# A two-layer diffusion block with a product-key expert layer: a group of four tokens weighed one token later, with ten ring slots

## The chip, the cores and the metric

One core of a Trainium2 chip. The time is that of one launch on the device in microseconds (us), from the runs shown; one execution is also profiled. Engines: TensorE (PE), VectorE (DVE), ScalarE (ACT), GpSimd (POOL) and SyncE (SP), which issues most weight loads. TensorE's clock has two levels, 1.2 and 2.4 GHz; a granted clock of 0.5 is the lower one.

## The reference

Two layers over 256 latent tokens with a context of 256 tokens, width 1024, all in float32. Each layer has a mixer (convolution, two kinds of attention, a Fourier mix, merged by gates) and then a layer of experts that is chosen by product keys. In the first layer the context tokens go through both; in the second only the latent ones do. So three sets of 256 tokens go through the experts, here called turns. The part that matters here is the end of the expert layer:

```
v1, i1 = top_k(s1, 16); v2, i2 = top_k(s2, 16)          # per token and head (8 heads)
cand = v1[..., :, None] + v2[..., None, :]
top_s, pos = top_k(cand, 16); eidx = cidx[pos]          # 16 of 16384 experts per head
g = softmax(top_s)
h = gelu(einsum('thkd,td->thk', eu[eidx], xc))          # 128 rows of 1024 per token
out = einsum('thk,thkd->td', g * h, ev[eidx])           # 128 more rows of 1024
```

For each token 128 experts are chosen. The rows `eu` of these are multiplied with the token and summed (128 numbers), the gelu of that times the softmax gives 128 weights, and the weighted sum of the 128 rows `ev` is the token's result.

## The kernel before

**Rows of experts.** A ring of ten slots (`SLOTS`) holds the rows of one token each: 128 partitions, one per chosen expert, with 1024 numbers of `eu` and 1024 of `ev`, 1 MB in all. GpSimd requests a token's rows with an indirect transfer (`ask`, L748) into slot `token % 10`. Before that it waits until the group whose token held the slot has been weighed (semaphore `weighed`).

**Per token.** TensorE broadcasts the token's 1024 numbers over the partitions of PSUM, in two halves of 512 (L1389; the operand `xr` holds the token as three bfloat16 parts, loaded by ScalarE's queue at L1827, two groups ahead). VectorE multiplies each half with the `eu` rows and sums it (L2535, which here is called a dot; it has two halves). The banks of the broadcast are a single pair, so a half of the next broadcast waits for the same half of the dot before (`dotted`). Only in the last 128 tokens of the third turn are there two pairs in turn (`x_bank`), and a broadcast waits for the dot two tokens back.

**Per group of four tokens.** After the fourth dot VectorE adds the halves (L2540), ScalarE takes the gelu (L1839), and VectorE multiplies with the softmax (L2545, `zcol`; semaphore `w_s`). VectorE waits for ScalarE in between and then goes on to the first dot of the next group. `weigh(g)` on TensorE is the weighted sum: eight matmuls with a weight of 32 columns (L1370), two halves for each of four tokens, that add to banks 6 and 7. Its last matmul raises `weighed`, which lets GpSimd request four more tokens. At the end of 32 groups (a tile of 128 tokens) ScalarE copies the sum out.

**Order.** Each engine's program is written out in a fixed order by a weaver (`Weave`): the steps of the layers (products, attention, norms, selection of experts) come in the order of `SCRIPT`, and between them tokens of the expert stream (`experts`) are put in, as many as the step's entry in `SHARE` grants. TensorE, VectorE, ScalarE and GpSimd use the same sequence, each with its part of a step and of a token. So a token stands between two steps of the layer, and where the steps have run out (`after` in the script) tokens follow each other directly. An engine works through its program in order: whatever stands behind a waiting instruction waits too.

Of the kernel before, what the change touches and what calls it, by code (L numbers as in the profile page):

```python
# [47 lines left out]
NR = NG // TT  # L48
# [177 lines left out]
def build(nc, x, ctx, ccols, cols_c, w_ada, w_rows, w_in, w_gate, w_out, w_q, w_key, b_in, nat_bias, gqa_sink, peer_uv0, peer_uv1,  # L226
          ident_c, wave_c, band_c, iota_c, strip_c, out):
    es = ExitStack()
    with es:
# [137 lines left out]
        def bank(i, a=0, b=512):  # L367
            return PS[:, i * 512 + a:i * 512 + b]
# [83 lines left out]
        def slot_of(q, n):  # L452
            whole = q * TOK + n
            return whole % SLOTS, 16 * (whole // SLOTS + 1)
# [34 lines left out]
        def x_bank(q, n):  # L489

            return 2 * (n % 2) if ORDER[q] == LAT1 and n >= P else 0
# [272 lines left out]
        def _(pe):  # L764
# [592 lines left out]
            def experts():  # L1357
                for q, f in enumerate(ORDER):
                    b = OF[f]
                    a = at_of["back", b]  # L1360

                    def weigh(g):
                        pe.wait_ge(w_s, q * NG + g + 1)
                        at = g % NR
                        if at == 0 and (q or g):
                            pe.wait_ge(y_out, 2 * q + g // NR)
                        for h in range(2):
                            for k in range(GRP):
                                slot, _ = slot_of(q, g * GRP + k)
                                last = T.matmul(PS[k * NR:(k + 1) * NR, (6 + h) * 512:(7 + h) * 512],  # L1370
                                                zcol[:, g % 2, k, NR - 1 - at:2 * NR - 1 - at],
                                                ring[:, slot, D + h * 512:D + (h + 1) * 512],
                                                start=(at == 0), stop=(at == NR - 1))
                        last.then_inc(weighed, 1)

                    for n in range(TOK):
                        g, k = n // GRP, n % GRP
                        whole = q * TOK + n
                        if n == 0:
                            pe.wait_ge(a["sel_s"], a.at("sel_s", 2))  # L1380
                        if k == 0:
                            pe.wait_ge(xr_land[g % 2], 16 * (q * NG // 2 + g // 2 + 1) * GRP)
                        for h in range(2):
                            if whole:
                                turns = 1 if n and x_bank(q, n) != x_bank(q, n - 1) else 0
                                if whole > turns:
                                    pe.wait_ge(dotted, 2 * (whole - turns) - 1 + h)
                            p0 = 32 * ((k + h) % GRP)
                            T.matmul(bank(x_bank(q, n) + h), onesb[p0:p0 + 3, :],  # L1389
                                     xr[p0:p0 + 3, g % 2, h * 512:(h + 1) * 512], start=True, stop=True)\  # L1390
                                .then_inc(xb_s, 1)
                        if k == 0 and g % NR:
                            weigh(g - 1)
                        if k == GRP - 1 and g % NR == NR - 1:
                            weigh(g)
                        yield
# [4 lines left out]
            for s_ in range(2):  # L1401
# [3 lines left out]
                last.then_inc(crow_p, 1)  # L1405
            woven["pe"] = Weave()
            woven["pe"].run(dict(ada=ada, norm=norm, front=front, early=early, part=part_, back=back, residual=residual), experts())

        @block.scalar
# [1269 lines left out]
```

## Time and profile before

| | |
|---|---|
| median of 3 runs | 3026.46 us (3022.73 to 3033.0) |
| profiled execution, its own time | 3031.7 us |
| its span in the trace | 3029.9 us |
| TensorE's mean granted clock | 0.785 |
| moved by the DMA engines | 1029.85 MB, mean 340 GB/s |
| requests of expert rows | 768, 805.36 MB |

How to read it. The span is the time from the first to the last recorded instruction. The busy time of an engine is the time in which it had at least one instruction in work; a share of 79% is an average over parts of the program with different limits. For a group of instructions, the idle time before them tells how long the engine had stood still, and the releaser is what ended most of that. The chain of waits starts at the last instruction and goes back to what released it. The DMA share is the mean busy share of the 16 DMA engines; at 1.0 a further transfer has to queue.

The three turns of the expert stream lie at about 470 to 1310 us, 1350 to 2110 us and 2320 to 3013 us. Up to 470 us and from 2140 to 2310 us no tokens are in work. From about 2460 us to the end there is next to nothing but tokens.

### The profile page before, as it was taken

How to read it: one execution, taken by the hardware profiler on the slowest of the kernel's cores; microseconds unless marked ns; L12 is line 12 of the kernel's file. 1: busy time of each engine (PE TensorE's matmuls, PEld its weight loads, DVE VectorE, ACT ScalarE, POOL GpSimd, SP SyncE). 2: the span in 40 equal slices, each digit the busy share in tenths (PEclk: the TensorE clock that was granted, in tenths of full speed). 3: DMA queues.
4: the chain of work that ended last, by engine and by line, in shares of the span. 5: the costliest groups of instructions: out<-in, count | busy, mean ns of one | idle time of the engine just before them, and what ended most of it. 6: DMA issues, size and time to landing. Idle time of an engine off the chain costs nothing.

```text
span 3029.9 us, 34666 instructions
## 1 busy us (share of the span) xinstructions
PE 2392.9 (79%) x11912; PEld 1305.4 (43%) x11912; DVE 1918.9 (63%) x6197; ACT 452.5 (15%) x1108; POOL 729.4 (24%) x779
## 2 busy tenths in 40 slices
PE   7989996878999878568989978878797566676556
PEld 6778892444556435113545543322685111121111
DVE  3879977876545557856864455665458855555555
ACT  2141120223100110012010012221221000000000
POOL 0000003232322222322322223332001333333332
PEclk8999996888999978667989987675898555655565
DMA  8628748998999988978999999999434989999996
GB/s 329 246 84 330 300 178 334 373 359 324 398 419 414 387 332 327 350 311 319 388 417 419 421 384 383 393 385 367 183 137 190 368 341 418 402 379 418 403 404 282
DMA packets 155375, 1029.85 MB, mean 340 GB/s; under 512 B 19136, under 2 KB 29888, under 8 KB 34496
## 3 DMA queue, kind: packets, MB, share of 16 engines
q0 software_dynamic: 110592, 805.36, 66.0%
q1 hardware_dynamic: 31648, 209.70, 17.7%
q10 hardware_dynamic: 12960, 12.59, 1.2%
q8 instruction: 94, 1.54, 0.2%
q14 instruction: 81, 0.66, 0.1%
HBM read 1018.66 MB, written 8.91 MB: 339 GB/s over the span
## 4 chain that ended last, share of the span: by engine, by line
PE 54%; DMA 19%; DVE 19%; issue 3%; ACT 2%; POOL 1%; ACTq 1%; SPq 0%; DVEq 0%; POOLq 0%
DMA ring<-in_peer_uv,eT 17%; PE PS L1370 14%; DVE ring L2535 9%; PE PS L930 7%; PE PS L1389 7%; PE PS L852 4%; PE PS L1041 4%; PE PS L951 2%; PE PS L971 2%; PE PS L1014 2%; DMA xr<-xrows 2%; PE PS L1223 1%; PE PS L854 1%; PE PS L815 1%; PE PS L1123 1%
## 5 line engine op out<-in xcount | busy, mean ns | idle before, releaser
L2535 DVE CUSTOM_DVE_ANT_0 ring<-ring,PS 128x512 f32<-128x512 f32 x1536 | 993.9, 685 | 783.3 <-PE PS L1389 600.5
L748 POOL DMA_INDIRECT ring<-in_peer_uv,eT x768 | 727.7, 947 | 2269.6 <-PE PS L1370 1422.2
L1389 PE MATMUL PS<-xr,onesb 3*128 3x512 bf16 x1536 | 527.7, 480 | 429.1 <-DVE hcol L2535 337.0
L1370 PE MATMUL PS<-ring,zcol 128*32 128x512 f32 x3072 | 579.1, 893 | 96.2 <-DVE zcol L2545 94.2
L1389 PEld LDWEIGHTS PS<-xr,onesb 3*128 3x128 bf16 x1536 | 105.2, 95 | 959.9 <-DVE hcol L2535 484.9
L1370 PEld LDWEIGHTS PS<-ring,zcol 128*32 128x32 f32 x3072 | 102.7, 142 | 379.2 <-issue 218.0
L930 PE MATMUL PS<-uT,W 128*128 128x256 f32 x1024 | 249.3, 393 | 0.0
L1839 ACT ACTIVATE ge<-hdot 128x4 f32<-128x4 f32 x192 | 39.4, 205 | 1263.0 <-DVE hdot L2540 1262.9
L930 PEld LDWEIGHTS PS<-uT,W 128*128 128x128 f32 x1024 | 193.6, 194 | 48.7 <-issue 22.2
L1912 DVE CUSTOM_DVE_ANT_0 ring<-ring 128x1024 f32<-128x1024 f32 x160 | 190.2, 1221 | 7.6 <-DMA ring<-in_w_rows 3.5
L852 PE MATMUL PS<-uT,W 128*128 128x256 f32 (+1 forms) x672 | 156.0, 386 | 8.6 <-ACT uT L1453 8.2
L852 PEld LDWEIGHTS PS<-uT,W 128*128 128x128 f32 x672 | 122.7, 200 | 41.8 <-issue 17.1
L971 PE MATMUL PS<-uT,W 128*128 128x256 f32 x512 | 133.5, 405 | 0.0
L2535 DVE DVE_READ_ACCUMULATOR2_ANT hcol<- 128x1 f32 x1536 | 126.6, 82 | 0.0
L1041 PE MATMUL PS<-uT,ring 128*128 128x128 f32 x1024 | 120.7, 280 | 5.7 <-DVE scratch L2388 5.7
L1041 PEld LDWEIGHTS PS<-uT,ring 128*128 128x128 f32 x1024 | 119.0, 196 | 6.1 <-DVE scratch L2388 6.1
L971 PEld LDWEIGHTS PS<-uT,W 128*128 128x128 f32 x512 | 95.7, 197 | 37.3 <-issue 26.1
L951 PE MATMUL PS<-mix,W 128*128 128x256 f32 x320 | 81.0, 385 | 0.0
L1941 DVE SCALAR_TENSOR_TENSOR mix<-hpad,cols,mix 128x256 f32<-128x256 f32 x180 | 77.5, 480 | 0.3
L1534 ACT ACTIVATE hpad<-PS,cols 128x256 f32<-128x256 f32 x64 | 30.4, 476 | 275.4 <-PE PS L951 274.3
L2545 DVE TENSOR_TENSOR zcol<-ge,gT 128x4 f32<-128x4 f32 x192 | 32.2, 167 | 58.9 <-ACT ge L1839 58.9
L951 PEld LDWEIGHTS PS<-mix,W 128*128 128x128 f32 x320 | 61.8, 194 | 9.7 <-issue 1.0
(362 smaller groups left out, 2287.0 us busy)
## 6 DMA issues: line engine op xcount, KB each, us to landing
ring<-in_w_rows SPq DMA_DIRECT2D x40, 1024.0 KB, 8.0
W<-in_w_in SPq DMA_DIRECT2D x30, 1024.0 KB, 9.5
W<-in_w_gate SPq DMA_DIRECT2D x16, 1408.0 KB, 8.0
W<-in_w_gate SPq DMA_DIRECT2D x16, 1280.0 KB, 7.7
W<-in_w_out SPq DMA_DIRECT2D x20, 1024.0 KB, 6.0
W<-in_w_gate SPq DMA_DIRECT2D x16, 1152.0 KB, 10.4
ring<-in_w_q SPq DMA_DIRECT2D x16, 1024.0 KB, 13.9
ring<-in_peer_uv,eT POOLq DMA_INDIRECT x768, 12.7
```

The lines of the kernel that those rows point to most:

```text
L748: pool.indirect_dma_start(ring[:, slot, :], None, (peer_uv0, peer_uv1)[b.l], bass.IndirectOffsetOnAxis(eT[:, f % 2, t:t + 1], 0)).then_inc ...
L852: last = T.matmul(bank(2 + n % 4, 0, r.nt * P), wk[:, blk * P:(blk + 1) * P], u_[:, k, r.cols], **go)
L930: T.matmul(bank(2 + n % 4, 0, TOK), wg[:, k, n % 2, :], uT[:, k, :], start=(k == 0), stop=(k == KD - 1))
L951: last = T.matmul(bank(2 + n % 4, TOK, 2 * TOK), W[:, slot, TILE + (at - first_kt + k) * P:TILE + (at - first_kt + k + 1) * P], yb[:, at + ...
L971: last = T.matmul(bank(2 + n % 4, 0, TOK), wg[:, k, g % 2, :], uT[:, k, :], start=(k == 0), stop=(k == KD - 1))
L1014: last = T.matmul(out_bank(m), W[:, slot, k * 2 * P + n % 2 * P:k * 2 * P + (n % 2 + 1) * P], mT[:, k, tt * P:(tt + 1) * P], start=(k == 0 ...
L1041: last = T.matmul(bank(2 + u % 2, 0, P), ring[:, u // 2, w0:w0 + P], uT[:, k, tt * P:(tt + 1) * P], start=(k == 0), stop=(k == KD - 1))
L1370: last = T.matmul(PS[k * NR:(k + 1) * NR, (6 + h) * 512:(7 + h) * 512], zcol[:, g % 2, k, NR - 1 - at:2 * NR - 1 - at], ring[:, slot, D + ...
L1389: T.matmul(bank(x_bank(q, n) + h), onesb[p0:p0 + 3, :], xr[p0:p0 + 3, g % 2, h * 512:(h + 1) * 512], start=True, stop=True)\
L1912: last = V.tensor_tensor_reduce(out=w_ if s_ else junk[:, c, :], in0=w_, in1=crow[:, s_, :], scale=1.0, scalar=0.0, op0=ALU.mult, op1=ALU.add,
L1941: ins = V.scalar_tensor_tensor(hacc[:, c, :], hpad[:, c, t:t + TOK], tap, hacc[:, c, :], ALU.mult, ALU.add)
L2535: V.tensor_tensor_reduce(out=u_half, in0=u_half, in1=bank(x_bank(q, n) + h), scale=1.0, scalar=0.0, op0=ALU.mult, op1=ALU.add, accum_out=h ...
```

## The change

In the expert stream of TensorE the weighing of the group before is put behind the broadcast of a group's second token (`k == 1`) instead of that of its first (`k == 0`). The last group of each tile of 32 is weighed behind its own last token, as before, so 186 of 192 weighings move. The number of slots, ten, is the same in both kernels, and no other engine's program changes.

```
                             T.matmul(bank(x_bank(q, n) + h), onesb[p0:p0 + 3, :],
                                      xr[p0:p0 + 3, g % 2, h * 512:(h + 1) * 512], start=True, stop=True)\
                                 .then_inc(xb_s, 1)
-                        if k == 0 and g % NR:
+                        if k == 1 and g % NR:
                             weigh(g - 1)
                         if k == GRP - 1 and g % NR == NR - 1:
                             weigh(g)
```

How TensorE's instructions stand now. First the start of the third turn, where the layer's steps have run out; a broadcast is two rows L1389, a weighing eight L1370. Before:

```order
L1000 MATMUL PS<-ident,uT 128x128 x8
L1077 MATMUL PS<-ident,small 128x128
L1389 MATMUL PS<-xr,onesb 128x512 x10
L1370 MATMUL PS<-ring,zcol 32x512 x8
L1389 MATMUL PS<-xr,onesb 128x512 x8
L1370 MATMUL PS<-ring,zcol 32x512 x8
```

After the change:

```order
L1000 MATMUL PS<-ident,uT 128x128 x8
L1077 MATMUL PS<-ident,small 128x128
L1389 MATMUL PS<-xr,onesb 128x512 x12
L1370 MATMUL PS<-ring,zcol 32x512 x8
L1389 MATMUL PS<-xr,onesb 128x512 x8
L1370 MATMUL PS<-ring,zcol 32x512 x8
```

Six broadcasts now stand before the first weighing instead of five; from there on both have four between two weighings.

Second, TensorE in the first attention part of layer 1 (`part`), where steps of the layer stand between tokens: L1268 and L1269 are products of queries and keys, L1279 turns the result, L1291 multiplies with the values. Before:

```order
L1389 MATMUL PS<-xr,onesb 128x512 x2
L1370 MATMUL PS<-ring,zcol 32x512 x8
L1268 MATMUL PS<-mix 128x256
L1269 MATMUL PS<-nkb_c,mix 128x128
L1268 MATMUL PS<-mix 128x256
L1269 MATMUL PS<-nkb_c,mix 128x128
L1389 MATMUL PS<-xr,onesb 128x512 x8
L1370 MATMUL PS<-ring,zcol 32x512 x8
L1279 MATMUL PS<-ident,scratch 128x128 x6
```

After the change, the same place:

```order
L1389 MATMUL PS<-xr,onesb 128x512 x2
L1268 MATMUL PS<-mix 128x256
L1269 MATMUL PS<-nkb_c,mix 128x128
L1268 MATMUL PS<-mix 128x256
L1269 MATMUL PS<-nkb_c,mix 128x128
L1389 MATMUL PS<-xr,onesb 128x512 x2
L1370 MATMUL PS<-ring,zcol 32x512 x8
L1389 MATMUL PS<-xr,onesb 128x512 x6
L1279 MATMUL PS<-ident,scratch 128x128 x6
```

The products of L1268 and L1269 now stand in front of the weighing, and so does one broadcast more. Of the six remaining broadcasts' rows, the L1279 behind them was behind a weighing before.

## Rows read from the trace of the kernel before

**Rows 1.** The page: busy time of two engines, share of the span, instructions.

```profile
PE 2392.9 (79%) x11912; PEld 1305.4 (43%) x11912; DVE 1918.9 (63%) x6197; ACT 452.5 (15%) x1108; POOL 729.4 (24%) x779
```

**Rows 2.** The page's costliest groups: busy us, mean ns of one, idle before, releaser.

```profile
L2535 DVE CUSTOM_DVE_ANT_0 ring<-ring,PS 128x512 f32<-128x512 f32 x1536 | 993.9, 685 | 783.3 <-PE PS L1389 600.5
L748 POOL DMA_INDIRECT ring<-in_peer_uv,eT x768 | 727.7, 947 | 2269.6 <-PE PS L1370 1422.2
L1389 PE MATMUL PS<-xr,onesb 3*128 3x512 bf16 x1536 | 527.7, 480 | 429.1 <-DVE hcol L2535 337.0
L1370 PE MATMUL PS<-ring,zcol 128*32 128x512 f32 x3072 | 579.1, 893 | 96.2 <-DVE zcol L2545 94.2
```

**Rows 3.** The chain of waits, by line: 2320 to 2480 us, then 2480 to 3000 us.

```profile
by line: PE PS L1370 26.4%; DVE ring L2535 21.1%; PE PS L1389 15.4%; issue 8.5%; DMA xr<-xrows 4.5%; DVE mix L2343 2.9%; DVE mix L2340 2.8%; DVE small L2050 2.2%; DVE small L2043 2.2%; DVE mix L2044 1.9%; DVE small L2047 1.7%; DVE mix L2342
...
by line: DMA ring<-in_peer_uv,eT 63.3%; PE PS L1370 17.8%; DVE ring L2535 5.8%; issue 5.0%; POOL ring L748 4.9%; PE PS L1389 2.3%; PE PS L815 0.7%; ACT ge L1839 0.7%; DVE hdot L2540 0.5%; DVE zcol L2545 0.5%; DVE X L2522 0.2%; DVE ysb L2518
```

**Rows 4.** Busy us by window (us, length, PE, PEld, DVE, ACT, POOL, PEclk, DMA share, GB/s).

```profile
480.00:540.00 60.00, 36.05 (x119) 6.35 (x118) 52.33 (x208) 1.36 (x6) 14.98 (x16) 0.56 1.01 408
540.00:800.00 260.00, 217.81 (x1082) 116.26 (x1084) 189.10 (x656) 73.45 (x168) 75.91 (x80) 0.85 0.90 355
1200.00:1310.00 110.00, 68.58 (x252) 17.81 (x252) 90.45 (x357) 8.41 (x19) 31.39 (x32) 0.65 0.86 334
1500.00:1800.00 300.00, 265.38 (x1282) 152.75 (x1280) 157.16 (x477) 34.69 (x77) 88.44 (x94) 0.93 1.01 415
1920.00:2110.00 190.00, 154.65 (x660) 54.93 (x656) 110.83 (x407) 45.56 (x102) 65.57 (x70) 0.64 0.99 398
2320.00:2460.00 140.00, 78.12 (x256) 14.19 (x260) 109.50 (x407) 5.58 (x16) 43.45 (x44) 0.57 0.88 349
2460.00:2690.00 230.00, 163.99 (x548) 28.53 (x540) 122.53 (x400) 5.54 (x23) 82.50 (x89) 0.57 1.01 409
2720.00:3000.00 280.00, 166.87 (x649) 29.57 (x649) 149.62 (x487) 5.54 (x27) 101.67 (x109) 0.58 1.01 407
```

**Rows 5.** The timeline from 2450 us: start, duration, instruction, idle before.

```profile
2450.11 0.17 DVE L2545 TENSOR_TENSOR zcol<-ge,gT 128x4 f32<-128x4 f32 x1 [1.99 <-ACT ge L1839]
...
2450.33 3.64 PE L1370 MATMUL PS<-ring,zcol 128*32 128x512 f32 x16 [1.75 <-DVE zcol L2545]
...
2451.19 0.68 DVE L2535 CUSTOM_DVE_ANT_0 ring<-ring,PS 128x512 f32<-128x512 f32 x1
...
2454.27 0.93 POOL L748 DMA_INDIRECT ring<-in_peer_uv,eT  x1 [10.88 <-PE PS L1370]
2454.65 0.69 DVE L2535 CUSTOM_DVE_ANT_0 ring<-ring,PS 128x512 f32<-128x512 f32 x1 [2.77 <-PE PS L1389]
...
2455.40 1.21 PE L1389 MATMUL PS<-xr,onesb 3*128 3x512 bf16 x2 [0.89 <-DVE hcol L2535]
...
2456.15 0.69 DVE L2535 CUSTOM_DVE_ANT_0 ring<-ring,PS 128x512 f32<-128x512 f32 x1 [0.20 <-PE PS L1389]
```

**Rows 6.** Requests of expert rows: asked in 2320 to 2460, then 2460 to 2690 us.

```profile
DMA to landing us min/median/max: 5.4/9.2/18.7
...
DMA to landing us min/median/max: 7.3/13.9/16.8
```

**Rows 7.** The timeline from 1962 us, in the first attention part of layer 1.

```profile
1962.22 3.64 PE L1370 MATMUL PS<-ring,zcol 128*32 128x512 f32 x16
1962.43 0.69 DVE L2535 CUSTOM_DVE_ANT_0 ring<-ring,PS 128x512 f32<-128x512 f32 x1 [1.27 <-PE PS L1389]
...
1965.79 1.23 PE L1268 MATMUL PS<-mix 64*128 64x256 f32 x4
...
1966.81 0.60 PE L1269 MATMUL PS<-gkc,mix 64*128 64x128 f32 x4
...
1967.87 0.69 DVE L2535 CUSTOM_DVE_ANT_0 ring<-ring,PS 128x512 f32<-128x512 f32 x1 [4.13 <-PE PS L1389]
...
1969.15 0.69 DVE L2535 CUSTOM_DVE_ANT_0 ring<-ring,PS 128x512 f32<-128x512 f32 x1
```

More of the change, by code:

```diff
@@ L1391, in experts @@
                                 .then_inc(xb_s, 1)
-                        if k == 0 and g % NR:
+                        if k == 1 and g % NR:
                             weigh(g - 1)
```

## The prediction

> **What bounds the kernel now.** I began with the page's engine line [rows 1]: TensorE is busy for 79% of the span and VectorE for 63%, so no compute engine bounds the whole. The costliest groups [rows 2] name the loop that the change touches. VectorE sat idle 783.3 us before its dot products at L2535, 600.5 us of it until a broadcast at L1389 came. TensorE lost only 96.2 us in front of the weighing matmuls at L1370, and GpSimd's requests at L748 waited 1422.2 us for a weighing to end. One could read the 600.5 us as the prize of the change. The next views say that most of it is not.
>
> The chain of waits [rows 3] differs by stretch. From 2320 to 2480 us weighings, dots and broadcasts take turns (26.4%, 21.1%, 15.4%). From 2480 us to the end a transfer of expert rows is 63.3% of the chain. The windows [rows 4] say why: the DMA share is 1.01 in 1500 to 1800, 2460 to 2690 and 2720 to 3000 us, and 0.99 in 1920 to 2110. It is 0.86 in 1200 to 1310 and 0.88 in 2320 to 2460. In the first kind of stretch, call it full, a group of four tokens can't go faster than its four requests land, whatever VectorE waits for. In the second kind, open, the loop between TensorE and VectorE sets the pace. GpSimd's counts over four give the groups: 23.5, 17.5, 22 and 27 in the four full windows, 8 and 11 in the two open ones. The first groups (480 to 540 us, 4 groups) have a share of 1.01 as well.
>
> **The change, part by part.** Nothing is added or removed. Of 192 weighings 186 move back by one token; the six at a tile's end stay. Each is priced in an open stretch, then in a full one.
>
> *Open stretch, one pair of banks.* The group at 2450 us [rows 5] shows the loop. The weights of the tokens are made at 2450.11, the weighing starts at 2450.33 and takes 3.64 us, and the next token's dot starts at 2454.65, 4.32 us after the weighing began, with 2.77 us of idle VectorE. The token after that starts at 2456.15. Now the new order on the same rows. The second half of the first token's dot starts at 2451.19; a broadcast follows the start of such a half by 0.75 us (2454.65 to 2455.40), so the second broadcast's last half starts at 2451.94 and, at the mean of 480 ns [rows 2], ends at 2452.4. Only then can the weighing start: 2.1 us later than before. The second token's dot is no longer behind it and runs beside it, which is what the change buys. The third token's dot then starts 4.32 us after 2452.4, at 2456.7, where it started at 2456.15. So VectorE's stall isn't removed but goes from the second token to the third, and the loop is **0.6 us longer** per group: the weighing used to start beside the first dot, and now has to wait for it and for a broadcast. The wait that the new place takes away, that for the weights at 94.2 us in all [rows 2], lies mostly in the last stretch, which is full. For 8 and 11 groups this is 19 x 0.6 = +11.4 us. Bounds: zero, if other work of VectorE lies in just the right gaps and hides it, and 0.6 on twice as many groups (+23), since 540 to 800 us with a share of 0.90 [rows 4] is partly open.
>
> *Steps of TensorE between tokens.* Where a step of the layer stands right behind the weighing, the move helps. At 1962 us [rows 7] the weighing (3.64 us) and two products (L1268, L1269) run in a row, VectorE idles 4.13 us, and the dots of the second and third token start at 1967.87 and 1969.15. In the new order the products run beside the first dot. It starts at 1962.43, its second half 0.6 us on, at 1963.05, so the weighing begins 0.75 + 0.48 later, at 1964.3, and the third dot 4.32 after that, at 1968.6: 0.5 us gained. The order of TensorE shows a step behind the weighing in 81 of 192 places, but most of them lie in full stretches or where TensorE has no idle time to give back. I count six such groups in open places: -3 us. Bounds: 0 and 30 x 0.5 = -15.
>
> *Requests.* GpSimd issues the next four when the weighing has ended (2453.97, request at 2454.27 [rows 5]), so each batch goes out 2.1 us later. Behind it on GpSimd's queue are only its other three. In a full stretch this is hidden by the transfers still in flight: a request there lands after 13.9 us in the median, 7.3 at least, while in the open one the least is 5.4 [rows 6]. The difference, 13.9 - 5.4 = 8.5 us, is queueing, and 2.1 of it can go before the transfers run dry. Cost per group: nothing. What isn't hidden is the entry into a full stretch: the last batch before it leaves the DMA engines idle 2.1 us longer, and all after it shifts. I count this twice, at 2460 us and at the entry of the full stretch at 1500 us: +4.2 us. Bounds 0 and, with five such entries, +10.
>
> *The last 128 tokens.* They use two pairs of banks, so the second broadcast doesn't wait for the first token's dot. The weighing isn't delayed and VectorE's stall does vanish there. But the share is 1.01 and the landing of the rows sets the pace: 0.
>
> *Other queues.* SyncE's weight loads and ScalarE's loads of the token's rows hang on marks of other steps or of the dots, not on these weighings. 0. If the full stretches had room, the row to watch would be the wait of a broadcast for those rows, which come next.
>
> **Sum:** 11.4 - 3 + 4.2 = +12.6 us on the profiled execution's own 3031.7 us. The median of the runs is 5.2 us lower, 3026.46; with the same difference I forecast **3039.0 us**.
>
> **Rivals.**
> 1. *All is hidden.* The full stretches are the greater part, and the open ones have further work of VectorE between tokens (90.45 of 110 us busy in 1200 to 1310, 109.5 of 140 in 2320 to 2460 [rows 4]) which may cover the later stall as well as the earlier. Against it: the chain in 2320 to 2480 runs through the weighings nevertheless [rows 3]. About 3027 us.
> 2. *Faster.* The effect at 1962 us [rows 7] counts in many places, since it also shortens stretches of the layer's own work, and the 0.6 us is covered. It decides once more than some 30 groups give 0.5 us: 3026.5 - 15 = 3011.5 us. Against it: TensorE is 265 of 300 us busy in 1500 to 1800, and transfers are full there.
> 3. *The ring runs dry.* Ten slots less a weighing's delay are too few, and the DMA engines idle in full stretches. It decides where the queueing of 8.5 us is less than the delay, as it may be beside bursts of weight loads. At worst 23.5 + 17.5 + 22 = 63 groups x 2.1 = +132 us; a third of that gives +44, or 3070 us. Against it: the least landing time in 2460 to 2690, 7.3 us, still lies above 5.4.
>
> Beside the third rival stands a rule of the Trainium skill ("DMA: Bandwidth & Descriptors", Rules for kernel authors): to overlap transfers with compute, issue the transfer early and wait for it late. The change issues every batch later, which by that rule is a loss in each group; the trace shows the rule's cost only where the DMA share falls below 1.
>
> **How the numbers follow.** A measurement of this kernel can tell about 0.3% (9 us) from no change. My forecast's mechanism has a chance of 0.47, of which 0.13 falls within 9 us; rival 1 has 0.22, rival 2 0.18 (0.15 of it over the bound), rival 3 0.13. That gives faster 0.15, same 0.38, slower 0.47. The range reaches from the faster case, 3012, to rival 3's 3070.
>
> **What would show it.** In the profile after: in 2320 to 2480 us the interval from one weighing to the next about 0.6 us longer, VectorE's stall behind a weighing on the third token of a group and not the second, and the start of the full stretch some 8 us later, with a share of 1.0 unchanged in it. From 2720 us on the groups should follow at the old rate although VectorE's waits for L1389 all but vanish. Waits of the dots for landed rows should grow by about what the waits for broadcasts lose. I am wrong if the share in a full stretch falls, if the early stretches (540 to 800 us) shrink by more than 10 us, or if TensorE's clock there, now 0.85 [rows 4], comes out different: the prices above are taken at the clock of before.

## The result, and the profile after

The kernel became slower: 3072.61 us in the median of four runs (3069.23 to 3073.87) against 3029.73 us before (four runs, 3022.73 to 3033.87). The ratio is **1.0137 (95%: 1.0122 to 1.0153)**, some +42 us where +12.6 was forecast, and just above the end of the range. The profiled execution has a span of 3072.0 us (3029.9 before) at the same mean clock, 0.786 and 0.785.

The page of the changed kernel, its engine line and the groups that answer to [rows 1, 2]:

```profile
PE 2400.1 (78%) x11912; PEld 1306.0 (43%) x11912; DVE 1919.0 (62%) x6197; ACT 453.2 (15%) x1108; POOL 728.1 (24%) x779
...
L2535 DVE CUSTOM_DVE_ANT_0 ring<-ring,PS 128x512 f32<-128x512 f32 x1536 | 994.1, 685 | 832.9 <-PE PS L1389 544.7
L748 POOL DMA_INDIRECT ring<-in_peer_uv,eT x768 | 726.4, 946 | 2313.2 <-PE PS L1370 1468.9
L1389 PE MATMUL PS<-xr,onesb 3*128 3x512 bf16 x1536 | 540.5, 482 | 519.2 <-DVE hcol L2535 358.6
L1370 PE MATMUL PS<-ring,zcol 128*32 128x512 f32 x3072 | 584.1, 901 | 18.0 <-DVE zcol L2545 17.1
```

The counts and VectorE's busy time are the same. The wait of the weighings for their weights is nearly gone (94.2 to 17.1 us), and so is a tenth of the dots' wait for broadcasts (600.5 to 544.7). But VectorE's idle time before the dots has grown from 783.3 to 832.9 us. TensorE's wait for dots before a broadcast grew, and GpSimd's requests wait 47 us longer for weighings.

The windows of the changed kernel, to be read against [rows 4] (us, length, PE, PEld, DVE, ACT, POOL, PEclk, DMA share, GB/s). The last three are moved by the 38 to 40 us that the kernel is late there:

```profile
540.00:800.00 260.00, 213.37 (x1017) 106.55 (x1017) 183.43 (x635) 72.75 (x164) 70.91 (x75) 0.81 0.86 337
1200.00:1310.00 110.00, 77.30 (x319) 29.77 (x311) 90.88 (x395) 5.95 (x17) 33.18 (x35) 0.72 0.87 340
1500.00:1800.00 300.00, 265.23 (x1272) 153.60 (x1271) 160.14 (x489) 33.40 (x76) 88.19 (x94) 0.94 1.00 411
1920.00:2110.00 190.00, 145.77 (x628) 55.34 (x624) 104.92 (x392) 49.97 (x111) 63.87 (x68) 0.63 0.95 377
2358.00:2498.00 140.00, 76.89 (x249) 13.76 (x249) 107.32 (x400) 5.37 (x15) 39.58 (x41) 0.55 0.86 336
2498.00:2728.00 230.00, 159.24 (x534) 28.42 (x533) 123.19 (x403) 5.70 (x24) 85.06 (x91) 0.60 1.00 406
2760.00:3040.00 280.00, 181.00 (x655) 33.88 (x651) 149.50 (x486) 5.54 (x27) 101.69 (x109) 0.59 1.00 403
```

The full stretches at 1500, 2498 and 2760 us still have a share of 1.00. The share fell in 540 to 800 us (0.90 to 0.86) and in 1920 to 2110 us (0.99 to 0.95). The second is one that the prediction had called full.

**Where the time went.** Number the groups of four tokens 0 to 191, 64 in a turn, and take the start of each group's L2545 in both traces. The difference, after minus before, is how late the changed kernel is there. It starts at 0.8 us at group 0 and ends at 42.4 us at group 191:

| groups | time before, us | what lies there | lateness gained, us | forecast, us |
|---|---|---|---|---|
| 0 to 12 | 486 to 646 | start of the first turn | +5.5 (3.7 of it in group 1) | 0 |
| 12 to 24 | 646 to 799 | attention, layer 0 | **+11.4** | 0 |
| 24 to 52 | 799 to 1202 | further steps | +5.5 | 0 |
| 52 to 60 | 1202 to 1307 | open | +0.4 | +4.8 |
| 60 to 68 | 1307 to 1413 | end of turn 1, start of turn 2 | **-5.9** | 0 |
| 68 to 108 | 1413 to 1919 | mostly full | +7.4 | +2.1 |
| 108 to 124 | 1919 to 2091 | attention, layer 1 | **+13.2** | 0 |
| 124 to 128 | 2091 to 2332 | end of turn 2 | -1.8 | 0 |
| 128 to 140 | 2332 to 2477 | start of turn 3, open | +5.4 | +8.7 |
| 140 to 191 | 2477 to 3014 | tokens alone, full | +0.5 | 0 |

The forecast's -3 us for steps of the layer was for six open groups that it didn't place. It is left out of the last column. The table says what the totals hide: the loop of tokens alone came out small, as forecast, and more than half of the loss, 24.6 of 42.4 us, was gained in the two attention parts, where steps of the layer stand between the tokens. And the change has real gains in it, around the end of the first turn. How far such a row can be trusted, two profiles of one and the same kernel tell (the one with eleven moved groups, below, which was run twice): they differ by 6.3 us over groups 0 to 12, by 2.6 over 124 to 128, and by at most 1.4 in every other row. So the rows of the attention parts stand well clear of it; the +5.5 us of the first row doesn't, except for the 3.7 us of group 1, which come back in another kernel below.

Within the two attention parts TensorE runs the same instructions in both kernels, so its time can be split into busy and idle:

| groups | TensorE busy, us | idle, us | granted clock |
|---|---|---|---|
| 12 to 24 | 127.3, then 134.3 | 26.6, then 30.9 | 0.82, then 0.81 |
| 108 to 124 | 139.6, then 139.5 | 31.7, then 44.9 | 0.65, then 0.64 |

In layer 1 the whole loss is time in which TensorE stands idle. In layer 0 the greater part, 7.0 of 11.4 us, is matmuls that took longer, and only 4.3 us is idle time.

**Was 1920 to 2110 us full?** The prediction called it so by its DMA share of 0.99. What the dots waited for in the kernel before, in that window (line, releaser: us in total, times, longest):

```profile
DVE ring L2535 <- PE PS L1389: 72.9, 40, 5.9
DVE ring L2535 <- DMA ring<-in_peer_uv,eT: 0.2, 1, 0.2
```

All of it was for broadcasts of TensorE and next to nothing for landed rows. In the other full windows at 1500 and 2460 us the waits for landed rows were 55.5 and 41.2 us. So in this one, in spite of its share, the landings did not set the pace.

**The open loop.** The first group of turn 3 behind its start, timeline of the changed kernel from 2368 us (start, duration, instruction, idle before):

```profile
2368.25 0.17 DVE L2545 TENSOR_TENSOR zcol<-ge,gT 128x4 f32<-128x4 f32 x1 [0.27 <-ACT ge L1839]
...
2371.20 0.69 DVE L2535 CUSTOM_DVE_ANT_0 ring<-ring,PS 128x512 f32<-128x512 f32 x1
...
2371.95 1.21 PE L1389 MATMUL PS<-xr,onesb 3*128 3x512 bf16 x2 [3.50 <-DVE hcol L2535]
...
2373.09 3.64 PE L1370 MATMUL PS<-ring,zcol 128*32 128x512 f32 x16
...
2377.41 0.69 DVE L2535 CUSTOM_DVE_ANT_0 ring<-ring,PS 128x512 f32<-128x512 f32 x1 [3.41 <-PE PS L1389]
```

The stall is now on the third token, and its dot starts 4.32 us after the weighing (2377.41 - 2373.09), the very distance of [rows 5]. This is the forecast's mechanism. Here it costs more than 0.6 us, though: the interval between two L2545, from group 128 to 129, is 15.0 us against 11.6 before. The same place before, from 2331 us:

```profile
2331.78 0.17 DVE L2545 TENSOR_TENSOR zcol<-ge,gT 128x4 f32<-128x4 f32 x1 [0.27 <-ACT ge L1839]
...
2332.00 3.64 PE L1370 MATMUL PS<-ring,zcol 128*32 128x512 f32 x16
...
2334.73 0.69 DVE L2535 CUSTOM_DVE_ANT_0 ring<-ring,PS 128x512 f32<-128x512 f32 x1
...
2336.24 0.69 DVE L2535 CUSTOM_DVE_ANT_0 ring<-ring,PS 128x512 f32<-128x512 f32 x1 [0.20 <-PE PS L1389]
```

Between the weights and the first dot VectorE works at a selection step (L2040 to L2050, 2331.86 to 2334.7), and the weighing, started at once, lay beside it. The stall of the dot behind was 0.20 us. In the new order TensorE stands idle through that step (3.50 us) and weighs afterwards. Where little of other work lies between the tokens, the loss is small as forecast: over groups 124 to 127 it is 0.5 us per group on average, over 138 to 140 0.65 us (single groups between 0.1 and 1.0).

**The attention part.** The waits of TensorE's matmuls there, in the columns used above. In the changed kernel, 1905 to 2147 us:

```profile
PE PS L1279 <- ACT scratch L1764: 7.3, 2, 3.8
...
PE PS L1291 <- ACT mix L1770: 2.0, 1, 2.0
```

In the kernel before neither row is there, in 1905 to 2147 us nor in 1866 to 2108. One of these places in the timeline of the changed kernel, from 2069 us (L2545 at 2069.49, the next at 2083.79, so an interval of 14.3 us):

```profile
2071.45 1.11 PE L1291 MATMUL PS<-mix 128*128 128x64 f32 x4 [1.99 <-ACT mix L1770]
...
2074.74 3.19 PE L1370 MATMUL PS<-ring,zcol 128*32 128x512 f32 x16
2074.95 0.69 DVE L2535 CUSTOM_DVE_ANT_0 ring<-ring,PS 128x512 f32<-128x512 f32 x1 [4.05 <-PE PS L1389]
...
2077.86 0.71 PE L1268 MATMUL PS<-mix 64*128 64x256 f32 x4
...
2079.25 0.69 DVE L2535 CUSTOM_DVE_ANT_0 ring<-ring,PS 128x512 f32<-128x512 f32 x1 [2.99 <-PE PS L1389]
```

And before, from 2034 us (L2545 at 2034.76 and 2046.63, 11.9 us):

```profile
2035.13 3.64 PE L1370 MATMUL PS<-ring,zcol 128*32 128x512 f32 x16
...
2038.70 0.75 PE L1291 MATMUL PS<-mix 128*128 128x64 f32 x4
...
2040.81 0.69 DVE L2535 CUSTOM_DVE_ANT_0 ring<-ring,PS 128x512 f32<-128x512 f32 x1 [4.16 <-PE PS L1389]
```

Before, the weighing covered ScalarE's copy L1770, and weighing and L1291 together made one stall of VectorE, 4.16 us. Now TensorE waits out the copy (1.99 us), which with L1291 alone makes a stall of 4.05 us, and the weighing makes a second one, 2.99 us, with another step (L1268) stacked on it. The parts of a step took longer as well (L1291 1.11 us against 0.75); TensorE had stood idle for 1.99 us before it, and had come straight from the weighing in the kernel before.

**The last 128 tokens.** What the dots waited for in the changed kernel, 2720 to 3000 us (same columns):

```profile
DVE ring L2535 <- DMA ring<-in_peer_uv,eT: 108.1, 93, 1.9
DVE ring L2535 <- PE PS L1389: 9.1, 5, 4.4
```

Before, in the same window:

```profile
DVE ring L2535 <- PE PS L1389: 65.6, 27, 3.1
DVE ring L2535 <- DMA ring<-in_peer_uv,eT: 56.4, 74, 1.2
```

The waits for broadcasts are all but gone, the waits for landed rows are longer by the same amount, and the groups come at the old rate (10.6 us each over groups 160 to 191 in both kernels). This is what the prediction said of this stretch.

### The profile page after: what moved, and what is told of

Same layout as the page of the kernel before. It is cut to its first block, busy times and chain, and to the rows that moved or that the text cites. A ratio compares the mean times of both kernels' runs of the same rounds, so it can differ in the third digit from the quotient of the medians.

```text
span 3072.0 us, 34666 instructions
## 1 busy us (share of the span) xinstructions
PE 2400.1 (78%) x11912; PEld 1306.0 (43%) x11912; DVE 1919.0 (62%) x6197; ACT 453.2 (15%) x1108; POOL 728.1 (24%) x779
## 4 chain that ended last, share of the span: by engine, by line
PE 54%; DVE 18%; DMA 17%; issue 6%; ACT 3%; POOL 1%; ACTq 1%; SPq 0%; DVEq 0%; POOLq 0%; another core or an unknown queue 0%
DMA ring<-in_peer_uv,eT 15%; PE PS L1370 13%; DVE ring L2535 9%; PE PS L1389 7%; PE PS L930 7%; PE PS L852 4%; PE PS L1041 4%; PE PS L951 2%; PE PS L1014 2%; PE PS L971 2%; DMA xr<-xrows 1%; PE PS L1223 1%; PE PS L854 1%; POOL ring L748 1%; PE PS L1123 1%
## 5 line engine op out<-in xcount | busy, mean ns | idle before, releaser
L2535 DVE CUSTOM_DVE_ANT_0 ring<-ring,PS 128x512 f32<-128x512 f32 x1536 | 994.1, 685 | 832.9 <-PE PS L1389 544.7
L1389 PE MATMUL PS<-xr,onesb 3*128 3x512 bf16 x1536 | 540.5, 482 | 519.2 <-DVE hcol L2535 358.6
L1370 PE MATMUL PS<-ring,zcol 128*32 128x512 f32 x3072 | 584.1, 901 | 18.0 <-DVE zcol L2545 17.1
L1389 PEld LDWEIGHTS PS<-xr,onesb 3*128 3x128 bf16 x1536 | 110.1, 95 | 1058.6 <-DVE hcol L2535 489.6
L930 PE MATMUL PS<-uT,W 128*128 128x256 f32 x1024 | 244.1, 387 | 0.0
L1370 PEld LDWEIGHTS PS<-ring,zcol 128*32 128x32 f32 x3072 | 103.6, 143 | 300.1 <-issue 266.1
L971 PE MATMUL PS<-uT,W 128*128 128x256 f32 x512 | 132.3, 403 | 0.0
L1223 PE MATMUL PS<-uT,W 128*128 128x256 f32 x256 | 70.0, 421 | 0.0
L2545 DVE TENSOR_TENSOR zcol<-ge,gT 128x4 f32<-128x4 f32 x192 | 32.4, 169 | 58.9 <-ACT ge L1839 50.8
## 6 DMA issues: line engine op xcount, KB each, us to landing
ring<-in_w_q SPq DMA_DIRECT2D x16, 1024.0 KB, 13.9
```

What stands on the lines that cost most here:

```text
L930: T.matmul(bank(2 + n % 4, 0, TOK), wg[:, k, n % 2, :], uT[:, k, :], start=(k == 0), stop=(k == KD - 1))
L971: last = T.matmul(bank(2 + n % 4, 0, TOK), wg[:, k, g % 2, :], uT[:, k, :], start=(k == 0), stop=(k == KD - 1))
L1223: last = T.matmul(bank(2 + u % 2, 0, TOK), W[:, slot, k * 2 * P + u % 2 * P:k * 2 * P + (u % 2 + 1) * P], uT[:, k, :], start=(k == 0), sto ...
L1389: T.matmul(bank(x_bank(q, n) + h), onesb[p0:p0 + 3, :], xr[p0:p0 + 3, g % 2, h * 512:(h + 1) * 512], start=True, stop=True)\
L2535: V.tensor_tensor_reduce(out=u_half, in0=u_half, in1=bank(x_bank(q, n) + h), scale=1.0, scalar=0.0, op0=ALU.mult, op1=ALU.add, accum_out=h ...
```

## The experiments

Three causes stood against each other. **P (place):** the weighing is a long piece on an engine that works in order. Between two tokens there is a gap, in which steps of the layer may stand. The weighing moved from the gap behind the first broadcast (gap A) to that behind the second (gap B). It costs time where gap A was empty and gap B has a step, and saves it in the reverse case. **R (requests):** the ring's slots come free later, so the transfers do. **U (uniform):** each moved group costs the same small amount wherever it stands, 43 us over 186 groups, or 0.23 us.

All edits are made to the kernel before. "Selector" is the condition `k == 0` at the weighing.

### Requests later, weighing in its old place

In `ask`, behind the wait for `weighed`, GpSimd also waits for a later dot:

```diff
                     pool.wait_ge(weighed, (whole - SLOTS) // GRP + 1)
+                    released = (whole - SLOTS) // GRP
+                    if released % NR < NR - 1:
+                        pool.wait_ge(dotted, 2 * ((released + 1) * GRP + 2))
```

> The order of TensorE is that of the kernel before (weighing behind the first broadcast); only GpSimd's requests are held back, until the second token of the next group has been dotted, some 2.0 us after the weighing has ended in the plain loop (2453.97 to 2455.98 us in the trace before). Theory P (place: what costs is where the weighing stands among the steps and broadcasts of TensorE): only the entries into full stretches cost, 0 to +10 us, ratio below 1.004. Theory R (ring: what costs is that slots come free later): at least two thirds of the change's 43 us, ratio 1.009 or more.

3044.83 us against 3031.28: 1.0052 (1.0035 to 1.0069), which is 13.5 us by the medians and 10.6 to 20.9 us by the interval. That lies between the two expectations: above P's, below R's. The first request of a batch left 6.66 us after the start of L2545 in the median of the groups, against 4.16 before and 5.97 in the changed kernel. So the experiment delays the requests somewhat more than the change does (2.5 against 1.8 us), and its cost is rather an upper bound for their part: about a third of the +42, at the end of the interval half of it. The page shows the new releaser (lines are three higher in this kernel):

```profile
L751 POOL DMA_INDIRECT ring<-in_peer_uv,eT x768 | 728.3, 948 | 2281.5 <-DVE hcol L2538 1362.7
```

The requests asked in 2466 to 2696 us, in the full stretch, landed sooner after being asked, to compare with the second row of [rows 6]:

```profile
DMA to landing us min/median/max: 9.0/12.1/16.3
```

The median is 12.1 us against 13.9: asked later, they queued shorter. That is the hiding the forecast spoke of. The lateness arises elsewhere, in groups 24 to 52 (+5), 76 to 84 (+3) and 128 to 150 (+4).

Its profiled execution, the fastest of the four, is 10.0 us longer than before. What decides is where this lateness does not arise. In the two attention parts this kernel delays the first request of a batch by 2.8 us in the mean in each, the change by 2.7 and 2.9. Yet over groups 12 to 24 and 108 to 124 this kernel lost nothing (-1.5 and -2.0 us), where the change lost 11.4 and 13.2. So the 24.6 us of the attention parts are not the requests'.

### Nine slots

```diff
-SLOTS = 10
+SLOTS = 9
```

> The kernel before with nine slots, so that each request goes out a token later than with ten while TensorE's order stays. Theory P: 0 to +12 us (entries into full stretches). Theory R: as much as the change or more, +40 us, ratio 1.013.

3044.66 us against 3031.28: 1.0041 (1.0027 to 1.0056), or +13.4 us, just above P's expectation and a third of R's. One slot less costs about what the later requests cost.

### Requests later still

As the first, with `GRP + 3` for `GRP + 2`: they wait for one token more.

> Order of the kernel before; the requests are held back until the third token of the next group has been dotted, some 3.5 us after the weighing in the plain loop, where the run with the second token had 2.0 us and +13.5 us in all. If each entry into a full stretch costs the delay: 13.5 x 3.5 / 2.0 = +24 us, ratio 1.008. If the transfers in flight were close to running dry in full stretches as well (theory R), more than twice 13.5: ratio 1.010 or more.

3066.84 us against 3028.91: 1.0126 (1.0110 to 1.0141). This is the second of its two expectations, in which the transfers run short. Requests leave 9.05 us after L2545, so the delay is 4.9 us, twice that of the first experiment, and the cost is 38 us by the medians (33 to 43 by the interval). The profiled execution was the fastest of its four and shows 29 us of it. Two of its windows (columns of [rows 4]), moved by the 15 and 26 us that the kernel is late there:

```profile
1515.00:1815.00 300.00, 262.11 (x1226) 148.68 (x1224) 149.74 (x461) 32.90 (x75) 84.06 (x90) 0.90 0.98 402
2486.00:2716.00 230.00, 162.90 (x536) 28.04 (x528) 121.80 (x396) 5.54 (x23) 83.35 (x89) 0.56 1.01 405
```

In the first of them a share that was 1.01 is 0.98; in the second, where there are next to only tokens, it is 1.01 as before. From group 144 on this kernel still gained no more than 1 us (27.5 to 28.5), and in the attention parts 1.1 and 2.4 us. Of its lateness, 8 us came in groups 24 to 48 and 11 in 72 to 96 (10.0 to 21.4). In these two stretches the weight loads share the DMA engines with the requests: their queue took 18.8% and 19.1% of the engines' time in 799 to 1202 and 1473 to 1782 us of the kernel before, and 0.2% from 2477 us on. There the dots now wait for landed rows: over groups 24 to 52 for 17.6 us before, 25.3 us with the first delay and 51.1 us with this one.

### The change in the attention parts alone, and elsewhere alone

```diff
-                        if k == 0 and g % NR:
+                        if k == (1 if 12 < q * NG + g < 21 or 101 < q * NG + g < 124 else 0) and g % NR:
```

> Moved only in the 30 groups that lie among the attention steps of TensorE (groups 13 to 20 and 102 to 123 of 192). Theory P: the differences of the group intervals of the two traces sum to +22 us there, so 3051 us, ratio 1.007. Theory U (uniform: each moved group costs 0.2 to 0.6 us wherever it stands): 30 x 0.23 = +7 us, ratio 1.002.

The second kernel moves all other groups:

> The complement: moved everywhere but in those 30 groups. Theory P: 43 - 22 = +21 us, ratio 1.007. Theory U: 156 x 0.23 = +36 us, ratio 1.012.

In the attention parts alone: 3045.46 us against 3031.28, 1.0055 (1.0037 to 1.0072). Elsewhere alone: 3052.91, 1.0068 (1.0051 to 1.0085). Both intervals hold P's ratio and exclude U's, though by the medians the first is +14 us where P said +22. The first kernel gains 13.8 us of lateness in groups 108 to 124, as the whole change does, but only 5.5 of the 11.4 in 12 to 24, and it wins 6.3 us back in 96 to 108. The second gains 3.4 to 3.6 us in groups 1, 39 and 129 each, and loses 3.3 to 3.6 in groups 61, 67 and 82. In 12 to 24 it gains 2.7 us itself, with eight of the twelve groups in their old order. The profiled spans are +13.0 and +26.9 us, together 39.9 against the 42.1 of the whole change; by the medians the two are +14 and +22, together 36 of 43. So the losses add up from places, and about 14 us of them come from 30 of the 186 groups.

### Picking by the gaps: first gap empty, second gap empty

By the order of TensorE's instructions alone I picked 12 groups with nothing in gap A and a step in gap B (14 to 20, 103, 109, 112, 118, 121) in which P expects a loss:

```diff
-                        if k == 0 and g % NR:
+                        if k == (1 if q * NG + g in (14, 15, 16, 17, 18, 19, 20, 103, 109, 112, 118, 121) else 0) and g % NR:
```

> Moved only in the 12 groups among the attention steps where TensorE has no step between the first and second token and one between the second and third (14 to 20, 103, 109, 112, 118, 121): the weighing leaves a gap of its own and joins a step in one gap. Theory P: each costs up to the length of a dot, 1.2 us, +8 to +14 us, ratio 1.003 to 1.005. Theory U: 12 x 0.23 = +3 us.

3052.05 us against 3030.34: 1.0068 (1.0047 to 1.0090). Twelve moved weighings cost 21 us (14 to 27), half of what 186 cost, and more than the 8 to 14 us that P expected; U's 3 us are out. The twelve intervals themselves are 20.3 us longer in its profile. In group 19 the timeline of this kernel, from 734 us, shows it:

```profile
734.50 2.79 PE L1370 MATMUL PS<-ring,zcol 128*32 128x512 f32 x16
...
737.22 1.92 PE L1123 MATMUL PS<-stage_c,scratch 128*128 128x128 f32 x8
739.07 0.66 PE L1139 MATMUL PS<-mix,gvb_c 128*64 128x128 f32 x8
739.66 0.39 PE L1389 MATMUL PS<-xr,onesb 3*128 3x512 bf16 x2
740.19 0.69 DVE L2535 CUSTOM_DVE_ANT_0 ring<-ring,PS 128x512 f32<-128x512 f32 x1 [3.98 <-PE PS L1389]
```

The kernel before, same place, from 728 us:

```profile
728.16 1.92 PE L1370 MATMUL PS<-ring,zcol 128*32 128x512 f32 x16
...
730.33 1.16 PE L1123 MATMUL PS<-stage_c,scratch 128*128 128x128 f32 x8
730.55 0.69 DVE L2535 CUSTOM_DVE_ANT_0 ring<-ring,PS 128x512 f32<-128x512 f32 x1 [0.87 <-PE PS L1389]
```

Before, weighing and attention step had a broadcast between them, so each overlapped with a dot, and VectorE waited 0.87 us. Now they run in a row and VectorE waits 3.98 us; the interval is 12.6 us for 9.6. The pieces themselves are longer too (2.79 for 1.92, 1.92 for 1.16). The granted clock was 0.92 in 730 to 736 us before, and 0.69 in 737 to 740 us of this kernel, after TensorE had been busy for only 3.51 of the 6 us in front. How much of the loss is the clock and how much the order isn't told apart.

The reverse, eight groups with a step in gap A and none in B:

```diff
-                        if k == 0 and g % NR:
+                        if k == (1 if q * NG + g in (104, 105, 106, 113, 114, 115, 122, 123) else 0) and g % NR:
```

> Moved only in the 8 groups of the layer-1 attention part where the step stands between the first and second token and none between the second and third (104, 105, 106, 113, 114, 115, 122, 123): the weighing leaves the step's gap for an empty one. Theory P: the opposite sign of the run with the first gap empty, -2 to -6 us. Theory U: +2 us. Both are near what a run can tell; the group intervals of the trace decide.

3031.68 us against 3030.34: 1.0004 (0.9994 to 1.0015). No gain: the interval holds U's +2 us and just excludes P's -2 to -6. Group 115 is 3.2 us shorter and 106 1.7, the others between -1.0 and +1.0. The eight intervals are 5.3 us shorter together, which is what P said, but groups among them that weren't moved grew (103 by 1.2 us, 119 by 2.5), and what was gained in 108 to 124 (1.5 us) was lost behind it. So P predicts the sign of the moved intervals here, and not what is left of it in the end.

The same rule can be put to the whole change, as a count made afterwards from the two traces. For each of the 186 moved groups, the order of TensorE tells whether a step stands in gap A and in gap B, and the two traces how much longer its interval became:

| gap A | gap B | groups | change of their intervals, us | per group |
|---|---|---|---|---|
| empty | step | 20 | +26.5 | +1.3 |
| step | empty | 18 | -15.2 | -0.8 |
| step | step | 61 | +16.2 | +0.3 |
| empty | empty | 87 | +17.1 | +0.2 |

Both signs come out as P has them. (The eight and the twelve groups of the last two experiments are among them: -2.9 and +14.1 us in the change.) For comparison, the kernel that only delays the requests has +1.5 and -5.2 us in the first two rows. The two rows in which P says nothing hold 33.3 us of the sum, though by little per group. The open loop, the requests and places like group 129, where a step of another engine decides, are candidates for them; how the 33.3 us divide isn't shown.

### The weighing behind the third broadcast

```diff
-                        if k == 0 and g % NR:
+                        if k == 2 and g % NR:
```

> The same step once more: the weighing behind the broadcast of the third token. Theory R (requests late): the requests go out another 1.5 to 3.3 us later and the loss more than doubles, ratio 1.03 or more. Theory P: the open stretches lose another 0 to 0.6 us per group only where a step is met, and the total is between that of the change and 1.5 times it, ratio 1.012 to 1.021.

3098.08 us against 3030.34: 1.0228 (1.0207 to 1.0248), +68 us, between the two and close above P's. Its requests leave 8.44 us after L2545, 4.3 us later than before, which is a little less than in the experiment that cost 38 us without moving any weighing. So here the requests may be half of the loss; no run tells their part from that of the place.

### Moved only where it was shorter

Since the local differences come back from kernel to kernel, I took the groups by measurement: eleven whose interval, from the group before to them, had been shorter with the weighing moved (by 1.4 to 3.6 us in ten of them; group 43 only in the kernel that moves elsewhere, by 3.2), and left the others as they were.

```diff
-                        if k == 0 and g % NR:
+                        if k == (1 if q * NG + g in (3, 43, 59, 61, 62, 67, 106, 115, 122, 131, 136) else 0) and g % NR:
```

> Moved only in 11 groups whose interval was shorter by 1.4 us or more with the move (3, 43, 59, 61, 62, 67, 106, 115, 122, 131, 136). Their differences sum to -29 us; some are only paybacks of a neighbour's loss, so theory P: -12 us (-5 to -29), 3019 us, faster than both kernels. Theory U: +2.5 us. Theory R: +1 us.

3008.61 us against 3030.34: **0.9932 (0.9909 to 0.9955)**. This is faster than both kernels. I ran it again on another chip:

> The kernel with 11 moved groups once more on the same chip as the one with 13: ratio 0.993 as before, and no difference between the two beyond 1 to 3 us.

3011.43 us against 3028.91: 0.9943 (0.9926 to 0.9960). In its profile the eleven intervals are 25.0 us shorter together, and the span 26.6. The groups had been picked from profiles of other runs on other chips, and the gain came back twice, so it isn't a chance of picking. With two more groups, 54 and 82:

> The 11 groups of the faster kernel and two more, 54 and 82, whose intervals were shorter by 1.4 and 3.3 us. 54 lies in an open stretch and 82 in a full one, where the landings set the pace: theory P expects -1 us from 54 and nothing lasting from 82, so the same as with 11 groups, ratio 0.993.

3005.12 us against 3028.91: **0.9920 (0.9906 to 0.9933)**, the fastest kernel measured; whether the two groups add anything is within the spread of the runs.

Group 61 shows what a gain is made of. The timeline before, from 1307 us, at the residual step (L815 turns the result on TensorE, L2508 and L2509 add it on VectorE):

```profile
1307.29 3.64 PE L1370 MATMUL PS<-ring,zcol 128*32 128x512 f32 x16
...
1310.86 2.52 PE L815 MATMUL PS<-ident,mod 128*128 128x128 f32 x16
...
1313.49 1.22 DVE L2508 TENSOR_TENSOR ysb<-ysb,PS 128x1024 f32<-128x1024 f32 x1 [5.00 <-PE PS L815]
```

And in the repeated run of the kernel with eleven groups moved, from 1297 us:

```profile
1297.49 3.78 PE L815 MATMUL PS<-ident,mod 128*128 128x128 f32 x16
...
1301.38 1.22 DVE L2508 TENSOR_TENSOR ysb<-ysb,PS 128x1024 f32<-128x1024 f32 x1 [2.59 <-PE PS L815]
1301.70 1.92 PE L1370 MATMUL PS<-ring,zcol 128*32 128x512 f32 x16
1302.64 1.23 DVE L2509 SCALAR_TENSOR_TENSOR ysb<-X,ysb 128x1024 f32<-128x1024 f32 x1
```

L815 comes first, VectorE waits 2.59 us for it instead of 5.00, and the weighing runs beside VectorE's two additions, where TensorE has nothing else to do. Whichever of the two comes first is the slow one: before, the weighing took 3.64 us and L815 2.52, now L815 takes 3.78 and the weighing 1.92. The granted clock in the 7 us in front was 0.50 in both. The interval is 12.5 us for 15.9.

## Why the prediction was wrong, step by step

- **Direction:** right, slower. **Size:** +12.6 forecast, +42 measured. That the direction was right is in part luck: the terms that were priced at a loss, the open loop and the requests, are the smaller part of what was measured.
- **"Open stretch, one pair of banks", +11.4:** the mechanism was right (the stall on the third token, 4.32 us behind the weighing, 0.5 and 0.65 us per group where tokens follow each other). As a sum it was too high: +5.4 us for groups 128 to 140, of which 3.4 are the selection step in group 129, and +0.4 for 52 to 60.
- **"Steps of TensorE between tokens", -3, bounds 0 and -15: this is the step that failed.** I looked at one place, [rows 7], where a step stood behind the old weighing, and concluded that the move could only help there. At that very place it did: the interval (group 113) is 11.7 us for 12.7. I never asked what stood in the gap to which the weighing goes, nor what the weighing had covered in the gap that it leaves. The term of -3 us became about +23: 42 less some 13.5 for requests and 6 for the open loop. That is a difference, not a measurement of its own, and with the end of the interval for the requests it is 15. Three readings stand by it. The attention parts gained 24.6 us, and requests delayed as much gained nothing there. Twelve groups picked by this rule cost 21 us. And in the change the 20 groups with an empty gap A and a step in gap B are 26.5 us longer, the 18 of the reverse kind 15.2 us shorter. The places are seen: a weighing joined to a step (3.98 us of stall for 0.87), a weighing that no longer covers ScalarE's copy (L1291, L1279: 9.3 us of waits of matmuls that weren't there) or VectorE's selection (+3.4 us in group 129). In layer 0, 7.0 of the 11.4 us are matmuls that took longer; how much of that the order caused through the clock stays open.
- **Which stretches are full:** 1920 to 2110 us had a share of 0.99 and was put at zero. It is made of such steps, and it gave +13.2 us (groups 108 to 124); its share fell to 0.95. Its dots had waited 0.2 us for landed rows and 72.9 us for broadcasts, so the landings left no room in which a loss of TensorE could hide. That row was in the trace of before.
- **"Requests", +4.2, bounds 0 and +10:** probably too low. The delay came out as forecast (1.8 us for 2.1), the hiding in the stretch of tokens alone too (+0.5 us over 51 groups), but a somewhat longer delay by itself (2.5 us) costs 13.5 us (10.6 to 20.9). What the change's own 1.8 us cost was not measured alone. The cost behind it lies mostly in stretches where weight loads share the DMA engines, which the forecast had not separated. The rule of the Trainium skill ("DMA: Bandwidth & Descriptors", Rules for kernel authors), to issue early and wait late, thus held here with +13.5 us for 2.5 us of lateness, gained in those stretches and hardly at all in the last one or in the attention parts.
- **"The last 128 tokens" and "Other queues", 0:** right. The waits went from broadcasts to landings (65.6 to 9.1, 56.4 to 108.1 us) with no change of rate. The wait of the broadcasts for the token's own rows, which the prediction named as the row to watch, grew from 54.7 to 84.0 us in all, but nearly the whole of that lies in the groups from 141 on (33.2, then 63.7 us), where the rate stayed.
- **Rivals:** the third's 3070 us is near the time measured, but for another reason. It had the transfers run dry in the full stretches, and the share stayed at 1.00 at 1500, 2498 and 2760 us. That something of it is real where weight loads are in flight, the second delay of the requests shows. Rival 2's mechanism is real in single groups (-3.4 us in group 61) and lost in the sum. Rival 1 is out.
- **The signs of error it had named:** the share in a stretch called full fell, and in 540 to 800 us the clock changed (0.85 to 0.81; over the same groups, 12 to 24, only 0.82 to 0.81). Both came true. That stretch grew where I had looked out for it shrinking.

## What to carry to other kernels

When a long piece moves along an engine that works in order, list for each place what stands in the gap it leaves and in the gap it enters, on every engine, and ask what it covered there: a wait of a step for another engine counts as much as a step. A uniform move averages gains and losses of the same size (here -3.6 to +4.0 us per group); the differences between group intervals of two traces show which places to keep, and keeping eleven or thirteen of 186 turned +1.4% into -0.6 to -0.8%. And before a stretch is called full by its DMA share, look at what the consumers wait for there: at a share of 0.99 they waited for TensorE alone, and the 13.2 us that it lost there were not hidden by the transfers.

## What the runs showed that I had not expected

Later requests cost more than entries into full stretches: 2.5 us later cost 13.5 us (10.6 to 20.9), 4.9 us later 38 (33 to 43). By the medians the cost grows faster than the delay, but the intervals also allow one in proportion. And the effect of moving one weighing is local and comes back: group 61 was 3.4, 3.5 and 3.4 us shorter in the profiles of the change, of the change outside the attention parts and of the eleven groups, group 129 3.4 us longer in the change and in the one outside the attention parts. It isn't so everywhere: groups 14 to 20 differ from before by up to 2.8 us one by one even where none of them moved, and there only their sum can be read (-1.2 to -1.5 us over groups 12 to 24 in the profiles that leave them all in place and keep ten slots, but for the second delay with +1.1).
